# Raw units, modulation and output projection of a two-block transformer kernel: instructions taken in another order

## What is computed

```python
sh1, sc1, g1, sh2, sc2, g2 = split(silu(c) @ w_ada + b_ada, 6)
u = rmsnorm(h, norm1_w) * (1.0 + sc1) + sh1
hq, hf, hi, hg, aq, ak, av = split(u @ w_in)         # four heads of 128 each
mix = concat(hgrn2(hq, hf, hi, hg), diff_attention(aq, ak, av)) @ w_out
h = h + g1 * mix
u = rmsnorm(h, norm2_w) * (1.0 + sc2) + sh2
h = h + g2 * (silu(u @ w_ffn_gate) * (u @ w_ffn_up)) @ w_ffn_down
return rmsnorm(h, final_norm_w)
```

## Time and profile before

| | |
|---|---|
| median of 3 runs | 1961.7 us (1959.49 to 1962.3) |
| the profiled execution's own time | 1961.08 us |
| its span in the trace | 1959.3 us (1.8 us of the time lie around it) |
| TensorE busy | 1902.6 us, 97% |
| VectorE, ScalarE, GpSimd busy | 1105.5, 910.2, 137.7 us |
| mean granted TensorE clock | 0.986 of full |

### The profile page before, as it was taken

The page is one execution under the profiler, slowest core; times in us unless marked ns, Lnnn a source line. Parts: engine busy times, 40 slices in busy tenths (PEclk is TensorE's granted clock), DMA queues, the critical chain, the costliest instruction groups (busy, mean ns, idle before and its releaser), DMA issues.

```text
span 1959.3 us, 25234 instructions
## 1 busy us (share of the span) xinstructions
PE 1902.6 (97%) x8978; PEld 1546.4 (79%) x8978; DVE 1105.5 (56%) x1666; ACT 910.2 (46%) x1517; POOL 137.7 (7%) x132
## 2 busy tenths in 40 slices
PE   7999999999999899999999999989999899999997
PEld 6777788888788677778888878878887678888886
DVE  5566554444466767755444456687776664444322
ACT  5555543232477544444434467656555343232322
POOL 0000020000012000011000012211011100000000
PEclk9999999999999999999999999989999889999998
DMA  3112123323366322223232345522122122323331
GB/s 137 65 64 64 43 89 105 96 96 96 129 193 194 105 89 95 88 75 101 88 105 86 105 167 186 191 66 64 61 71 66 53 86 86 107 86 104 89 96 67
DMA packets 56482, 193.68 MB, mean 99 GB/s; under 512 B 7137, under 2 KB 7649, under 8 KB 56417
## 3 DMA queue, kind: packets, MB, share of 16 engines
q1 hardware_dynamic: 47712, 163.60, 26.0%
q0 software_dynamic: 7696, 27.79, 4.4%
q10 hardware_dynamic: 1008, 1.45, 0.2%
HBM read 186.52 MB, written 2.10 MB: 96 GB/s over the span
## 4 chain that ended last, share of the span: by engine, by line
PE 91%; DVE 4%; ACT 2%; issue 1%; DMA 1%; SPq 0%; ACTq 0%; POOL 0%; DVEq 0%
PE ps L369 26%; PE ps L370 26%; PE ps L371 26%; PE ps L2192 1%; PE ps L2070 1%; PE ps L1070 1%; PE ps L2051 1%; PE ps L2086 1%; PE ps L1095 1%; PE ps L1085 1%; DVE wlo L351 1%; PE ps L2074 1%; PE ps L2240 0%; PE ps L2227 0%; PE ps L2266 0%
## 5 line engine op out<-in xcount | busy, mean ns | idle before, releaser
L369 PE MATMUL ps<-xh,whi 128*128 128x512 f32 x1536 | 610.1, 397 | 4.0 <-ACT h L1248 2.0
L370 PE MATMUL ps<-xl,whi 128*128 128x512 f32 x1536 | 601.6, 392 | 0.0
L371 PE MATMUL ps<-xh,wlo 128*128 128x512 f32 x1536 | 601.4, 392 | 0.0
L351 DVE TENSOR_TENSOR wlo<-raw,whi 128x1024 fp32r<-128x1024 f32 (+1 forms) x296 | 368.1, 1250 | 190.9 <-ACT whi L340 184.4
L340 ACT ACTIVATE whi<-raw 128x1024 fp32r<-128x1024 f32 (+1 forms) x304 | 311.7, 1035 | 168.3 <-PE ps L371 167.9
L369 PEld LDWEIGHTS ps<-xh,whi 128*128 128x128 f32 x1536 | 291.0, 189 | 69.8 <-issue 2.7
L370 PEld LDWEIGHTS ps<-xl,whi 128*128 128x128 f32 x1536 | 291.0, 189 | 61.2 <-issue 2.2
L371 PEld LDWEIGHTS ps<-xh,wlo 128*128 128x128 f32 x1536 | 290.6, 189 | 61.5
L369 PE MATMUL ps<-acth,whi 128*128 128x512 f32 x528 | 211.2, 400 | 0.0
L370 PE MATMUL ps<-actl,whi 128*128 128x512 f32 x528 | 206.7, 391 | 0.0
L371 PE MATMUL ps<-acth,wlo 128*128 128x512 f32 x528 | 206.2, 391 | 0.0
(11 more groups left out here) (316 smaller groups left out, 2269.2 us busy)
## 6 DMA issues: line engine op xcount, KB each, us to landing
raw<-in_gu SPq DMA_DIRECT2D x132, 512.0 KB, 3.3
raw<-in_down SPq DMA_DIRECT2D x48, 512.0 KB, 3.7
raw<-in_qkv SPq DMA_DIRECT2D x24, 512.0 KB, 4.4
wada<-in_ada POOLq DMA_DIRECT2D x24, 512.0 KB, 3.8
tmps<-in_ada POOLq DMA_DIRECT2D x24, 512.0 KB, 3.6
raw<-in_qkvb SPq DMA_DIRECT2D x24, 512.0 KB, 3.6
raw<-in_down SPq DMA_DIRECT2D x24, 384.0 KB, 3.1
raw<-in_recur SPq DMA_DIRECT2D x16, 512.0 KB, 3.4
```

Of the source, the lines that this page charges most:

```text
L351: eng.tensor_tensor(wlo[:, s, 0:n], raw[:, s, 0:n], whi[:, s, 0:n].bitcast(F32), ALU.subtract).then_inc(lo_done, 1)
L369: pe.matmul(ps[:, bank], whi[:, s, w], hi[:, k0 + k], start=start and k == 0, stop=False)
L370: pe.matmul(ps[:, bank], whi[:, s, w], lo[:, k0 + k], start=False, stop=False)
L371: mm = pe.matmul(ps[:, bank], wlo[:, s, w], hi[:, k0 + k], start=False, stop=stop and k == n - 1)
```

## The change

It replaces one addition on POOL by a product with ones on TensorE (part 6), and otherwise takes the same instructions in another order:

1. `shift_products` stands behind the second raw unit instead of in the first (both places).
2. VectorE modulates right behind the norm's factor; `raw_out("f")`, `biases` and `stage_norm` come after it. ACT's `gate_out` comes after `modulate_act`.
3. First pair: ACT copies i to hv (a new semaphore `first_input`) right behind `gate_log`; the root for the second norm (into `oraw`), `shift_high` and the splits of the units after i and g are moved on ACT; on VectorE the split "i" goes ahead of the scan, the split "g" ahead of two levels, and `refine_rest` and `shift_low` to the round t = 0.
4. Round t = 3: VectorE takes `mix_shares`, `head_var`, then the two splits of `mix`.
5. `mix`: the splits of its fifth and sixth units come at j = 0 and j = 2 of the first four; the factor on tile m + 1 (`regained`) comes behind the addition of tile m; ACT makes xh ahead of the square, but for the last tile.
6. POOL adds up seven squares; TensorE takes the eighth by a matmul of its own (`two_totals`).

Parts of the diff, with the lines that are only carried through left out:

```diff
@@ res_act / res_dve (split at j = 0 and 2; xh ahead of the square)
-                    if not leading(t) or j >= begun:
+                    if begun == 2 and sooner and leading(t):
+                        if j % 2 == 0:
+                            split_hi(act, u, (1, j // 2), freed=3)
+                    elif not leading(t) or j >= begun:
                         split_hi(act, u, ahead(u, t, j, end))
...
                         residual_hi(act, r, m, gain)
+                        last = end and j == u.body - 1
+                        if raw is not None and not last:
+                            raw_hi(act, r, m, raw)
                         residual_sq(act, r, m, (j // per) % 2)
-                        if raw is not None:
+                        if raw is not None and last:
                             raw_hi(act, r, m, raw)
...
+        def regained(dve, m, gain):
+            dve.scalar_tensor_tensor(h[:, m], h[:, m], column(gain, m), rstd[:, :], ALU.mult, ALU.mult)\
+               .then_inc(n_scaled["x"], 1)
...
                         if regain is not None:
-                            dve.scalar_tensor_tensor(h[:, m], h[:, m], column(regain, m), rstd[:, :],
-                                                     ALU.mult, ALU.mult).then_inc(n_scaled["x"], 1)
                             dve.wait_ge(n_scaled["x"], m + 1)
...
+                        if regain is not None and m < KT - 1:
+                            regained(dve, m + 1, regain)
                         residual_lo(dve, r, m, gain)
@@ raw_ffn_pe
+            def two_totals():
+                wait(pe, r.added, KT)
+                pe.matmul(ps[:, 7], ones[:, :], sqsum[:, :], start=True, stop=False)
+                wait(pe, r.squared, KT)
+                pe.matmul(ps[:, 7], ones[:, :], sq[1], start=False, stop=True).then_inc(r.total.sem, 1)
...
-            product(pe, u, 0, 0, 0, xh, xl, ready=r.x_lo, midway=lambda: total(pe, r, 7),
-                    late=lambda: shift_products(pe, u, 1, 5))
+            product(pe, u, 0, 0, 0, xh, xl, ready=r.x_lo, midway=two_totals)
             wait(pe, r.h_new, 6)
             product(pe, u, 0, 1, 1, xh, xl, read=raw_read)
+            shift_products(pe, u, 1, 5)
@@ dense (PE): the same for duo, and
-                if last_in[bank] is not None:
+                if (kind, t) == ("v", 0):
+                    pe.wait_ge(first_input, 1)
+                elif last_in[bank] is not None:
@@ block.scalar, loop over t
                     gate_inverse(n)
                     if n == 0:
-                        act.wait_ge(n_lo["1"], KT)
-                        root(act, r1f)
-                        wait(act, r1f.root, 2)
-                        shift_high(act, 1)
+                        high("i", 0)
...
                     gate_log(n)
+                if n == 0:
+                    act.wait_ge(mm_done, u.number(0, UNIT_OF["i", 0]) + 1)
+                    act.activation(hv, ps[:, BANK_OF["i"]], ACT.Copy).then_inc(first_input, 1)
+                if t == 0:
+                    wait(act, r1f.rstd, 4)
...
                     decays(n, 3)
+                if n == 0:
+                    act.activation(oraw[:, :], var[:, :], ACT.Ln).then_inc(r1f.root.sem, 1)
+                    wait(act, r1f.root, 1)
+                    act.activation(oraw[:, :], oraw[:, :], ACT.Exp, scale=-0.5).then_inc(r1f.root.sem, 1)
+                    shift_high(act, 1)
@@ block.vector
-            raw_out("f", 2, kd)
-            biases(dve, 0, 5, -1.0)
-            modulate_dve(dve, "1", scale1, 0, twin, (tmp[3], tmp[4]))
...
+            modulate_dve(dve, "1", scale1, 0, twin, (tmp[3], tmp[4]))
+            biases(dve, 0, 5, -1.0)
+            raw_out("f", 2, kd)
+            stage_norm()
...
-                else:
+                if t >= 0 and more:
+                    head_var(2 * t, 3)
+                    mix_shares(t)
+                elif t >= 0:
+                    mix_shares(t)
+                    head_var(2 * t, 3)
                     split_lo(dve, U["mix"], (0, 2), in_turn=True)
                     split_lo(dve, U["mix"], (0, 3))
```

More of the change, by code:

```diff
@@ L409, in build, with __init__ @@
             counts = [0] * 8
-            def __init__(self, summed=True, scaled=True, alone=True):
+            def __init__(self, summed=True, scaled=True, alone=True, added=KT):
                 (self.h_new,
@@ L420, in __init__ @@
                  ) = (Since(s, n) for s, n in zip(Residual.sems, Residual.counts))
-                more = (KT * summed, KT * scaled, KT * scaled, KT * alone, (KT + 1) * alone, 1 * alone, 2, 4)
+                more = (KT * summed, KT * scaled, KT * scaled, KT * alone, (added + 1) * alone, 1 * alone, 2, 4)
                 Residual.counts = [n + m for n, m in zip(Residual.counts, more)]
@@ L425, in build @@
         r1a, r1f = Residual(), Residual(alone=False)
-        r2a, r2f = Residual(), Residual(scaled=False)
+        r2a, r2f = Residual(added=KT - 1), Residual(scaled=False)
         def residual_hi(act, r, m, gain):
@@ L714, in pipelined, with res_act @@
             stage_b(count - 1)
-        def res_act(act, u, r, gain, rooted=True, begun=0, ada=None, raw=None, extra=None):
+        def res_act(act, u, r, gain, rooted=True, begun=0, ada=None, raw=None, extra=None, sooner=False):
             per = 1 if u.body == 4 else 3
@@ L746, in body @@
                 for j in range(u.body):
-                    if not leading(t) or j >= begun:
+                    if begun == 2 and sooner and leading(t):
+                        if j % 2 == 0:
+                            split_lo(dve, u, (1, j // 2))
+                    elif not leading(t) or j >= begun:
                         split_lo(dve, u, ahead(u, t, j, end))
@@ L1046, in lower_dve, with modulate_act @@
                                      xh[:, m].bitcast(F32), ALU.add, ALU.subtract).then_inc(n_lo[key], 1)
-        def modulate_act(act, key, shift, tmp, u, between=None):
+        def modulate_act(act, key, shift, tmp, u):
             for m in range(KT):
-                if m == 3 and between is not None:
-                    between()
                 act.wait_ge(n_scaled[key], m + 1)
@@ L1221, in _ @@
             pool.wait_ge(rc.scan, HG)
-            pool_squares(pool, r2a, None)
+            pool_squares(pool, r2a, None, tiles=KT - 1)
             pool_squares(pool, r2f, r2a, tiles=KT - 1)
@@ L1366, in query_out @@
                 act.wait_ge(raw_scaled, 2)
-                act.activation(hq[:, :], qd[:, :], ACT.Identity, bias=bias[:, 1:2]).then_inc(duo_out, 1)
-            modulate_act(act, "1", 0, (tmp[3], tmp[4]), u, gate_out)
+                act.activation(hq[:, :], qd[:, :], ACT.Identity, bias=bias[:, 1:2]).then_inc(duo_out, 2)
+            modulate_act(act, "1", 0, (tmp[3], tmp[4]), u)
             def high(kind, t):
@@ L1479, in _ @@
                         high("q", n)
+                    else:
+                        high("g", 0)
                 if t >= 0:
@@ L1502, in _ @@
                     decays(n, 2)
-                    wait(act, turned, 2 * n)
-                    unit_out("i", n, ACT.Copy, hv)
+                    if n:
+                        wait(act, turned, 2 * n)
+                        unit_out("i", n, ACT.Copy, hv)
                     decays(n, 3)
+                if n == 0:
[3 more added lines that the diff above has]
+                    shift_high(act, 1)
+                if t >= 0 and more:
+                    high("g", n)
                 if more:
-                    high("g", n)
                     act.preload_act_table_set(SILU)
@@ L1968, in _ @@
                 if more:
-                    level(n, (1, 2))
-                    low("g", n)
+                    if n:
+                        level(n, (1, 2))
+                        low("g", n)
+                    else:
+                        low("g", n)
+                        level(n, (1, 2))
                     level(n, (3,))
@@ L2162, in dense @@
                 if j == 0:
-                    product(pe, u, 0, j, 2, xh, xl, ready=r1f.x_lo, midway=lambda: twin_totals(pe),
-                            late=lambda: shift_products(pe, u, 0, 5))
+                    product(pe, u, 0, j, 2, xh, xl, ready=r1f.x_lo, midway=lambda: twin_totals(pe))
                     for part_of in (4, 5):
```

46 lines of the change are left out of this document (27 added, 19 removed).

## The result

| | before | after |
|---|---|---|
| median, same chip | 1960.60 us (1959.09 to 1962.3, 4 runs) | **1939.63 us** (1937.19 to 1941.35, 4 runs) |
| ratio | 1 | 0.9892, 95% interval 0.9875 to 0.9909 |
| the profiled execution | 1961.08 us, span 1959.3 | 1937.19 us, span 1935.3 |

The change brings 21.0 us, 16.2 were forecast. The interval lies clear of 1, so the kernel is faster.

A forecast was written before the change was run, and what follows sets the result against it. TensorE was taken as the bound (busy 1902.6 of 1959.3 us), so only its waits and half clock could be won: 6.5 + 4.0 + 7.5 - 1.8 = 16.2 us, from 1961.08 to 1944.9 us, range 1939 to 1953.

The forecast's parts named there:

- I charge one fall, 1.8: Clock term: of the new waits of 2.0, 1.9 and 2.0 us, one is followed by half clock, costing 1.8 us.
- the first new wait: First pair: unit d waits 2.0 us for ACT's evacuation of g from its bank.
- the forecast's second new wait: First pair: the level scores wait 1.9 us for the first pick, VectorE's last level product being late.
- Part 1: First pair: hv's wait and half clock go, new waits come; gain 6.7 us, taken as 6.5.
- part 2: Round t = 3: shares ahead of splits remove a wait of 2.2 and 1.8 of half clock, 4.0 us.
- Part 3: Output projection: 13.9 us to be won, less 6.0 of waits and 0.4 for starts, 7.5 gained.
- 0.4 for the starts: Output projection: 0.4 us lost for the starts behind four waits.
- ports don't collide: Rival, chance 0.15: no VectorE-GpSimd collision in the projection, which gains 10.7 us, and the clock holds; 1939.9 us.
- VectorE bounds the projection: Rival, chance 0.12: each VectorE instruction held up once, round 6.0 us against TensorE's 5.45; projection gains 3, 1949.4 us.
- Bank 6 takes hv's place: Rival, chance 0.06: g evacuated hardly sooner, new wait 4 us with a fall; first pair gains 2.5, 1948.9 us.
- The one on the slower side: Rival, chance 0.03: many short waits keep the projection at half clock, 4.8 us more per unit; six units give 1973.7 us.
- The change doesn't bring its order about: Rival, chance 0.02: another wait on the same semaphores holds hv or the split where they were; 1961 us.

The follow-up runs named there:

- A and B: Trace stretches: A from the norm's total ahead of the first pair to the head's sum in t = 3 (before 261.44 us), B onward behind all changes (80.81).
- the second profile of after: Also called the control: the changed kernel once more, unedited, beside the kernel before on one chip; 1939.58 us, ratio 0.9889.
- the version with the addition first: Changed kernel, projection's tile 0 added ahead of the fifth unit's split, ACT's sixth-unit split ahead of tile 1's square; 1938.04 us, 0.9887.
- that with the short shift product: Changed kernel with the shift product of only one of eight tiles (4 narrow matmuls instead of 32 in each place); 1938.32 us, 0.9901.
- both further gains: Two edits of the changed kernel: ACT's second-norm root and shift high part behind g's evacuation (1937.10 us), and the projection's addition ahead of the split (1938.04 us).

## Why the prediction was right and where it failed

Right by its own steps:
- **The wait for hv** is gone, and d's wait for g took its place. Here are hv's copy, q's copy, ACT's load of a table and the evacuation of g, against the earlier trace rows:

```profile
1290.23 0.58 ACT L1495 ACTIVATE tmps<-ps 128x512 f32<-128x512 f32 x1
...
1293.67 0.72 ACT L1388 ACTIVATE hq<-qd,small 128x512 f32<-128x512 f32 x1 [0.41 <-DVE qd L1785]
...
1298.06 1.28 ACT L1542 ACT_TABLE_LOAD   x1
1299.35 0.60 ACT L1399 ACTIVATE hgate<-ps 128x512 f32<-128x512 f32 x1
```

  q's copy to evacuation takes 5.7 us (5.8 to 6.0 told). q's copy came 1.5 us sooner than before beyond the early start of 2.7 (2.1 told).
- **The round t = 3:** 4.0 told, 4.04 found (from the level scores to the head's sum 212.04 before, 208.00 after), and 4.0 lost with the part undone.
- **The rounds** take 57.3 us each as before (from level scores to level scores), and so passed the first pair's gain on.
- **Which waits** stay in the projection: a start on the new h, two splits, the last square. But the two for splits sum to 1.65 us, where three with 4 to 5 were told as the sign.

That the time came out inside the range is in part luck: the errors 1 to 3 below all go the same way and reach its lower end.

The forecast was 16.2; with its terms against the second profile of after (20.3 in A and B) four things are left over, 4.1 us in sum.

1. **"I charge one fall, 1.8"** failed. The control has no fall behind the first new wait (1.00 from 1302.90 on), after has one, and A differs by 0.2 us. Two mechanisms are in it. Unit d starts 35.07 us behind the norm's total in both, though the half clock behind the shift product took 3.4 us in one and 6.8 in the other: TensorE being later, its wait is 1.5 instead of 3.0. Behind d, where no fall comes, the level scores wait 1.0 us for the first pick, which is the forecast's second new wait (1.9 told); where one comes, it fills that time. All seven profiles in which d waits 2.9 to 3.0 us bear it out: five have a fall behind it and A from 250.6 to 251.8, two have none and A at 250.35 (the two of the five at 251.7 and 251.8 are those in which VectorE's modulation ended 1.0 and 1.3 us later). TensorE doesn't set the end of the first pair; ACT, and VectorE beside GpSimd's splits, do. The forecast added a clock price to a stretch where it had itself found TensorE waiting. **1.8 us.**
2. **Part 1 and part 2 together, "6.5" and "4.0"**: A gained 11.1 in the control. A size, **0.6 us**.
3. **Part 3, "6.0" of waits**: they sum to 3.3 (1.09, 0.50, 1.15, 0.53). I had set an addition of 1.27 us against each split or factor as a whole, but GpSimd's addition starts behind the square, and by then VectorE is not yet at its next instruction: it meets the last 0.4 to 0.6 us. The Trainium skill's rule (page "SBUF — State Buffer", section "Who interferes with whom"), that the earlier of two such instructions holds the other off, agrees with every pair of rows above, and the constant written by GpSimd, which reads nothing, held nothing off. What failed was my timetable of who starts when. Worth **2.7 us** of the forecast; all collisions together cost 1.7. The forecast's case without collisions has a slip of its own: 13.9 less 3.0 and 0.4 is 10.5, not 10.7.
4. **"0.4 for the starts"**: the second total (1.0 us, L928) was left out of the sum, though the change's sixth part adds it. What is left of B, 1.4 in place of 0.4, is this and the starts, **1.0 us** the other way.

The first profile of after has 1.6 us more of gain in B than the control, by the shorter half clock behind the second shift product (3.4 against 6.8 us; the kernel before had 6.8). Nothing in the change does this: versions with the same code there had either.

Busy and idle time were told wrongly, 5 to 6 and 10 to 11, and were 12.1 and 11.9. The shift product's half clock, told as unchanged, was half as long at both places in after (3.4 us gained by chance), up to 1.7 each came from the stretches at 532 and 673 us, and the shift products took 3.49 us at full clock where they had 4.04 and 3.81.

Of the rivals, *ports don't collide* came closest in number (1939.9) and is false: without any addition read by GpSimd the kernel is 1.7 us faster still in B. *VectorE bounds the projection* is true up to the seventh unit (the order of the splits changed nothing) and false as a price. *Bank 6 takes hv's place* is false: g is evacuated 3.6 us sooner even without the early start (1305.65 to 1299.35, less 2.7). The one on the slower side is refuted: the clock held at 1.00 through four waits of 0.5 to 1.15 us. *The change doesn't bring its order about* is false: the wait for hv is gone.

Open: why a stretch at half clock takes 3.4 or 6.8 us in the same code, and why one follows d's wait of 3.0 us in after but not the same wait in the version with the addition first or in that with the short shift product. Open too is the share of part 2 and of the rest of part 3. A version with both further gains (1.2 in A, 1.1 in B) wasn't tried.

## What to carry to other kernels

Price a fall of the clock only where TensorE's own work sets the end of the stretch; where it waits for another engine further on, that wait takes the fall up. A collision costs what is left of the other engine's instruction at the moment when yours starts, so write down both start times before you charge it, and look for the order that puts your instruction at its end. Work that doesn't depend on the late data (here the narrow products of the shift) is nearly free if it stands where the matrix engine would wait for that data: taking out 3.1 us of it, and the half clock behind, gained nothing at one place and 0.8 to 2.4 us at the other.

## What the hardware showed that I had not expected

- Half clock followed the narrow matmuls, though TensorE counts as busy throughout them (3.49 of 3.49 us). With 32 of them all twelve profiles of the changed kernel and its versions show it behind the second place, and ten of them behind the first. With 4 in place of 32 the one profile shows none between 1255 and 1610 us, in spite of waits of 3.0, 1.2 and 1.1 us and of up to 0.5 for each of ten tiles. One profile is little for the first place, where two of the twelve had none either.
- Of TensorE's waits between 1255 and 1610 us, none of 1.9 us or less had half clock right behind it in any profile. The one of 2.0 (old order within a tile), those of 2.2 for the shares, the 2.7 for the one total, and all of 3.6 us and more had it. That of unit d, 2.9 to 3.0 us, had it in five of seven.
- The stretches at half clock came in two lengths, about 3.4 and 6.8 us, in executions of the same kernel.
- Two level products of 128x256, 0.41 us each when alone, took 1.62 and 2.59 us beside GpSimd's splits of 2.41 and 2.55 us.
